# Attention inside a gated-delta-rule stage: both heads of a pair in one step, by row and column groups of the array

## The chip, the core and the metric

The kernel runs on one core of a Trainium2 chip. Its time is the device time of one execution in microseconds (us). Before the change it is 2827.43 us, the median of 3 runs (2822.66 to 2828.75).

The engines are TensorE (PE; its weight loads are listed as PEld), VectorE (DVE), ScalarE (ACT), GpSimd (POOL) and the queue that starts most transfers (SP). Each works through its own instructions in order; they wait for one another by semaphores.

## The reference, cut to what matters

Two transformer-like layers follow each other on x of 1 x 1024 x 1024 (float32). The first mixes tokens in two ways side by side: four heads of a gated delta rule, and eight heads of dilated attention, 64 channels each. The change touches only the attention:

```
for window, dil in ((128, 1), (512, 4), (2048, 16)):
    # query t sees keys t, t-dil, ..., t-window; scores are q.k / 8
    num, den, m = band_attention(...)
out = (w0*num0 + w1*num1 + w2*num2) / (w0*den0 + w1*den1 + w2*den2)   # w_i = exp(m_i - max m)
```

The kernel computes the same as one causal softmax over all keys: scores + strip, where the table strip holds log(how many of the three patterns hold this key), or -1e30. Then

```
x = x + concat(gated_delta_rule(...), attention) @ w_out
```

## The kernel before

**The three stages.** The first stage (0 to about 397 us) projects x. The second (397.9 to about 869 us) runs the gated delta rule and the attention together. The third (the rest) is matmuls with split weights: output projections, feed-forward layers and the second block. The change is within the second stage.

**The second stage** goes over 8 chunks of 128 tokens (`c` = 0..7) for the delta rule. A chunk inverts four 128x128 triangular matrices by six levels: `("corner", l)` is a set of four matmuls LT x T (L1613 on the tensor queue), which DVE masks into U (L1246); `("join", l)` is two sets of four matmuls (L1613), which DVE subtracts from T (L1251) and TT (L1253). After that come `read`, `solve` and `update` (L1697, L1698), the new state St (L1263), and the decays of the next chunk (L1628, the first matmul that needs St). Chunk `c` is worked in turn `i = c // 2`, `p = c % 2`.

**The attention** fills the gaps between the levels. Pair `i` of heads (four pairs) is done in chunks 2i and 2i+1: head `p` of the pair in chunk 2i+p. For each head it goes over the 8 query tiles h = 0..7 of 128 tokens; tile h has h+1 key blocks of 128 (causal). For a tile:

- `("scores", h)`: matmuls of 64 rows (the head's channels, at partitions 64p on) into PSUM banks 3 and 4 (L1721); DVE adds strip, takes the row maximum (L1300) and negates it (L1305); ACT takes the exponential in place in `sm` with row sums (L877).
- `("weigh", h+1)`: TensorE transposes the weights block by block (L1732) and ACT copies them to `pt` (L884). `("weigh", h+2)`: matmuls of the transposed weights (stationary) with values `vb`, 64 columns moving (L1744); DVE takes the reciprocal of the row sum (L1310) and scales the result into `ob` (L1313).
- `heads`, once per pair (after chunk 2i+1): 8 transposes of `ob` (L1706), a copy by ACT into `hh` (L862), the remainder by DVE into `hl` (L1273). `values` at the start of chunk 2i: 8 transposes (L1656) and a copy by ACT into `vb` (L843).

**What sets the order.** The list `ORDER` is written by hand; each engine walks it once per chunk and issues its own part of every stage. Chunks 0, 1, 6 and 7 are written out, chunks 2 to 5 are a loop over i = 1, 2.

```
ORDER = ["values", "turn_back", ("scores", 0), "pairs", "mix", "invert", ("scores", 1), ("weigh", 1)]
for l in range(1, LEVELS):
    ORDER += [("corner", l), ("scores", l + 1), ("join", l), ("weigh", l + 1)]
ORDER += ["begin", "read", ("weigh", 8), "solve", ("weigh", 9), "update", "load", "heads", "gram", "root"]
```

**Around the levels.** `turn_back` and `pairs` need ACT's copies knT and qnT (L847, L849), DVE's LT and AT (L1239, L1241), the masked U and the first T (L1287, L1289). `mix` finishes the delta rule's output of the chunk before (u at L1215, hh at L829, hl at L1220). ACT loads a function table twice in each chunk: for the square root (L870) and for the exponential (L877).

Of the kernel before, what the change touches and what calls it, by code (L numbers as in the profile page):

```python
# [326 lines left out]
def program(nc, a, out):  # L327

    ctx = ExitStack()
    with ctx:  # L330
# [35 lines left out]
        with ExitStack() as z:  # L366
            strip, lmask = sb("strip", [P, S], where=z), sb("lmask", [P, LEVELS + 1, P], where=z)
            ch = sb("ch", [P, 2, 16, P], where=z)
            qkvb = sb("qkvb", [P, 3, S], where=z)
            vb = sb("vb", [P, TT, P], where=z)  # L370
            G = {n: sb(n, [P, GH, P], where=z) for n in
                 "bm E gam kn qn v knT qnT kd qd ke LT AT T TT U u St Sg oz".split()}
            G["og"] = G["u"]
            cc = sb("cc", [P, 2, T_N], where=z)
            oc = sb("oc", [P, 8, GH], where=z)
            sm = sb("sm", [P, 2, S], where=z)
            pt = sb("pt", [P, 2, HALF], where=z)
            ob = sb("ob", [P, TT, P], where=z)
            ac = sb("ac", [P, 4, 16], where=z)
# [90 lines left out]
        def final_bank(a, t):  # L470
# [9 lines left out]
            on_ready ot_mm oh_ready s_mm s_max s_neg s_exp p_mm p_evac pv_mm rd_ready ob_ready obt_mm  # L480
            obh_ready obl_ready
# [31 lines left out]
        ORDER = ["values", "turn_back", ("scores", 0), "pairs", "mix", "invert", ("scores", 1), ("weigh", 1)]  # L513
        for l in range(1, LEVELS):
            ORDER += [("corner", l), ("scores", l + 1), ("join", l), ("weigh", l + 1)]
        ORDER += ["begin", "read", ("weigh", 8), "solve", ("weigh", 9), "update", "load", "heads", "gram", "root"]

        def turns(eng, turn):

            for p in range(2):  # L520
                turn(0, p, p == 0, False)
            with eng.Fori(1, TT // 2 - 1) as i:
                for p in range(2):
                    turn(i, p, False, False)
            for p in range(2):
                turn(TT // 2 - 1, p, False, p == 1)
# [7 lines left out]
        def _(sp):  # L534
# [56 lines left out]
            for i in range(1, 4):  # L591
# [3 lines left out]
                sp.wait_ge(s["s_mm"], 16 * i)  # L595
# [133 lines left out]
        def _(act):  # L729
# [102 lines left out]
            act.sem_inc(s["p_evac"], 2)  # L832
# [3 lines left out]
            def turn(i, p, first_chunk, last):  # L836
                c = 2 * i + p
                g0 = 24 * i + 12 * p
                for stage in ORDER:
# [20 lines left out]
                    elif stage == "heads" and p == 1:  # L860
                        act.wait_ge(s["obt_mm"], i + 1)
                        A(hh[:, bass.ds(4 + i, 1), :].rearrange("p a s -> p (a s)"),  # L862
                          PS[:, 3:5, :].rearrange("p a b -> p (a b)"), ACT.Copy).then_inc(s["obh_ready"], 1)
# [9 lines left out]
                    elif stage[0] == "scores" and stage[1] < 8:  # L873

                        h, n = stage[1], P * (stage[1] + 1)
                        act.wait_ge(s["s_neg"], 16 * i + 8 * p + h + 1)
                        A(sm[:, h % 2, 0:n], sm[:, h % 2, 0:n], ACT.Exp, bias=ac[:, 1, 8 * p + h:8 * p + h + 1],  # L877
                          accum_out=ac[:, 2, 8 * p + h:8 * p + h + 1]).then_inc(s["s_exp"], 1)
                    elif stage[0] == "weigh" and stage[1] <= 8:

                        for g, n in groups(stage[1] - 1):
                            act.wait_ge(s["p_mm"], g0 + g + 1)
                            act.wait_ge(s["pv_mm"], g0 + g + 1)
                            A(pt[:, g % 2, 0:n * P], PS[:, 5 + g % 2, 0:n * P], ACT.Copy).then_inc(s["p_evac"], 1)  # L884
# [164 lines left out]
        def _(dve):  # L1049
# [138 lines left out]
            dve.sem_inc(s["s_max"], 1)  # L1188
            dve.sem_inc(s["ob_ready"], 1)
            dve.sem_inc(s["obl_ready"], 1)  # L1190
# [37 lines left out]
            def turn(i, p, first_chunk, last):  # L1228
                c = 2 * i + p
                g0 = 24 * i + 12 * p  # L1230
                for stage in ORDER:
# [39 lines left out]
                    elif stage == "heads" and p == 1:  # L1271
                        dve.wait_ge(s["obh_ready"], i + 1)
                        TTo(hl[:, bass.ds(4 + i, 1), :].rearrange("p a s -> p (a s)"),  # L1273
                            PS[:, 3:5, :].rearrange("p a b -> p (a b)"),
                            hh[:, bass.ds(4 + i, 1), :].rearrange("p a s -> p (a s)").bitcast(F32),
                            ALU.subtract).then_inc(s["obl_ready"], 1)
# [15 lines left out]
                    elif stage[0] == "scores" and stage[1] < 8:  # L1292

                        h, n, k = stage[1], P * (stage[1] + 1), 8 * p + stage[1]
                        dve.wait_ge(s["s_mm"], 16 * i + k + 1)
                        if h >= 2:
                            dve.wait_ge(s["p_mm"], g0 + groups(h - 2)[-1][0] + 1)

                        V_.memset(small[:, 255:256], 0.0)
                        V_.tensor_tensor_reduce(out=sm[:, h % 2, 0:n],  # L1300
                                                in0=PS[:, 3:5, :].rearrange("p a b -> p (a b)")[:, 0:n],
                                                in1=strip[:, S - n:S], scale=1.0, scalar=-3e38, op0=ALU.add,
                                                op1=ALU.max, accum_out=ac[:, 0, k:k + 1]).then_inc(s["s_max"], 1)
                        dve.wait_ge(s["s_max"], 16 * i + k + 2)
                        TS(ac[:, 1, k:k + 1], ac[:, 0, k:k + 1], -1.0, None, ALU.mult).then_inc(s["s_neg"], 1)  # L1305
                    elif stage[0] == "weigh" and stage[1] >= 2:

                        h, k = stage[1] - 2, 8 * p + stage[1] - 2
                        dve.wait_ge(s["s_exp"], 16 * i + k + 1)
                        V_.reciprocal(ac[:, 3, k:k + 1], ac[:, 2, k:k + 1]).then_inc(s["rd_ready"], 1)  # L1310
                        dve.wait_ge(s["rd_ready"], 16 * i + k + 1)
                        dve.wait_ge(s["pv_mm"], g0 + groups(h)[-1][0] + 3)
                        TS(ob[:, h, 64 * p:64 * p + 64], PS[:, 7, 0:64], ac[:, 3, k:k + 1], None, ALU.mult)\  # L1313
                            .then_inc(s["ob_ready"], 1)
# [172 lines left out]
        def _(pe):  # L1487
# [148 lines left out]
            def mix(c):  # L1636

                pe.wait_ge(s["on_ready"], c + 1)
                pe.wait_ge(s["ob_ready"], 8 * c + 9)
# [3 lines left out]
            pe.sem_inc(s["pv_mm"], 2)  # L1643
# [3 lines left out]
            def turn(i, p, first_chunk, last_chunk):  # L1647
                c = 2 * i + p
                g0 = 24 * i + 12 * p
                for stage in ORDER:  # L1650
                    if stage == "values" and p == 0:

                        pe.wait_ge(pair_loaded, 16 * (i + 1))
                        pe.wait_ge(s["obl_ready"], i + 1)
# [48 lines left out]
                    elif stage == "heads" and p == 1:  # L1703
                        pe.wait_ge(s["ob_ready"], 16 * (i + 1) + 1)
                        for t in range(TT):
                            last = tr(PS[:, 3 + t // 4, (t % 4) * P:(t % 4 + 1) * P], ob[:, t], ident[:])  # L1706
                        last.then_inc(s["obt_mm"], 1)
# [5 lines left out]
                    elif stage[0] == "scores" and stage[1] < 8:  # L1713
                        h, n = stage[1], P * (stage[1] + 1)
                        pe.wait_ge(s["s_max"], 16 * i + 8 * p + h + 1)
                        if p == 0 and h == 0:
                            pe.wait_ge(s["vb_ready"], i + 1)
                        rows_ = slice(64 * p, 64 * p + 64)
                        for lo in range(0, n, HALF):
                            hi = min(n, lo + HALF)  # L1720
                            last = mm(PS[:, 3 + lo // HALF, 0:hi - lo], qkvb[rows_, 0, h * P:h * P + P],  # L1721
                                      qkvb[rows_, 1, lo:hi], start=True, stop=True)
                        last.then_inc(s["s_mm"], 1)
                    elif stage[0] == "weigh":
                        if stage[1] <= 8:
                            h = stage[1] - 1
                            pe.wait_ge(s["s_exp"], 16 * i + 8 * p + h + 1)
                            for g, n in groups(h):
                                pe.wait_ge(s["p_evac"], g0 + g + 1)
                                b0 = 4 * (g - groups(h)[0][0])  # L1730
                                for b in range(n):
                                    last = tr(PS[:, 5 + g % 2, b * P:b * P + P],  # L1732
                                              sm[:, h % 2, (b0 + b) * P:(b0 + b) * P + P], ident[:])
                                last.then_inc(s["p_mm"], 1)
                        if stage[1] >= 2:
                            h = stage[1] - 2
                            pe.wait_ge(s["ob_ready"], 16 * i + 8 * p + h + 1)
                            if h == 0 and not first_chunk:
                                pe.wait_ge(s["og_ready"], c)
                            for g, n in groups(h):  # L1740
# [138 lines left out]
def groups(h):  # L1879

    if h < 4:
        return [(h, h + 1)]
# [26 lines left out]
```

## Time and profile before

| | |
|---|---|
| median of 3 runs | 2827.43 us |
| profiled execution | 2822.73 us, span 2821.1 us |
| PE busy | 2645.8 us (94%) |
| DVE busy | 1640.6 us (58%) |
| ACT busy | 1061.7 us (38%) |
| POOL busy | 121.1 us (4%) |
| mean granted TensorE clock | 0.973 |

A float32 matmul is two records on PE and two on PEld; a transpose is one. The time of one is best read from the chain of work, where a piece is the advance that it made, and not from its duration, since matmuls overlap. The granted clock is a share of the full rate: 1.00 is 2.4 GHz, 0.50 is 1.2 GHz. Chunk boundaries are taken here at L1628, the decays of the next chunk.

### The profile page before, as it was taken

To read this page: it belongs to the slowest core of one execution; us is meant where nothing else is said; L and a number is where in the kernel's file an instruction comes from. 1 tells how busy PE (TensorE), PEld (TensorE's weight loads), DVE (VectorE), ACT (ScalarE), POOL (GpSimd) and SP (SyncE) were. 2 spreads that over 40 slices of the span, in tenths; PEclk is the share of its full clock that TensorE was granted. 3 is DMA by queue.
4 is the path that set the end of the run, shared out by engine and by line. 5 is a ranking of instruction groups with operands and counts; after the bars stand their busy time and mean duration, and the time that the engine had idled before them with its cause. 6 is when DMAs were issued, how large, how long until landed. Compare 5 with 4: busy or idle time off the path is not lost.

```text
span 2821.1 us, 32692 instructions
## 1 busy us (share of the span) xinstructions
PE 2645.8 (94%) x12696; PEld 2168.0 (77%) x12696; DVE 1640.6 (58%) x2458; ACT 1061.7 (38%) x1602; POOL 121.1 (4%) x123
## 2 busy tenths in 40 slices
PE   6999979999997999999999999988999999999998
PEld 5888767777776878878777877776887788788886
DVE  4124335556553566666665888656588864655555
ACT  3123323333332444433544344444433343433332
POOL 1000011112110000000000000000000000000000
PEclk9999989999998999999999999999999999999999
DMA  5222230111104323333223222222332233243332
GB/s 190 91 84 81 75 105 16 38 38 30 38 1 127 97 81 92 98 92 95 89 76 88 85 90 90 83 83 67 91 90 82 83 103 103 75 129 97 97 90 75
DMA packets 299293, 235.05 MB, mean 83 GB/s; under 512 B 8095, under 2 KB 275476, under 8 KB 299028
## 3 DMA queue, kind: packets, MB, share of 16 engines
q1 hardware_dynamic: 293684, 209.57, 25.1%
q0 software_dynamic: 5472, 23.60, 2.1%
q8 instruction: 92, 1.51, 0.2%
q14 instruction: 45, 0.37, 0.0%
HBM read 210.07 MB, written 23.07 MB: 83 GB/s over the span
## 4 chain that ended last, share of the span: by engine, by line
PE 78%; DVE 12%; ACT 4%; issue 3%; DMA 2%; SPq 1%; POOLq 0%; POOL 0%; ACTq 0%; DVEq 0%
PE PS L1781 11%; PE PS L1783 11%; PE PS L1782 11%; PE PS L1503 11%; PE PS L1613 7%; PE PS L1797 5%; PE PS L1798 5%; PE PS L1799 5%; PE PS L1721 3%; DVE wl L1063 3%; PE PS L1744 2%; DVE x L1346 1%; DVE cg L1450 1%; PE PS L1732 1%; ACT wh L737 1%
## 5 line engine op out<-in xcount | busy, mean ns | idle before, releaser
L1781 PE MATMUL PS<-hh,wh 128*128 128x512 f32 x1728 | 686.0, 397 | 6.7 <-DVE hl L1322 4.4
L1063 DVE TENSOR_TENSOR wl<-raw,wh 128x1024 fp32r<-128x1024 f32 x352 | 427.7, 1226 | 447.6 <-ACT wh L737 447.4
L1783 PE MATMUL PS<-hh,wl 128*128 128x512 f32 x1728 | 676.6, 392 | 0.0
L1782 PE MATMUL PS<-hl,wh 128*128 128x512 f32 x1728 | 676.3, 391 | 0.0
L737 ACT ACTIVATE wh<-raw 128x1024 fp32r<-128x1024 f32 x352 | 367.1, 1056 | 536.3 <-PE PS L1799 401.0
L1781 PEld LDWEIGHTS PS<-hh,wh 128*128 128x128 f32 x1728 | 326.8, 189 | 79.2 <-DVE hl L1322 5.5
L1782 PEld LDWEIGHTS PS<-hl,wh 128*128 128x128 f32 x1728 | 326.6, 189 | 71.3 <-issue 4.3
L1783 PEld LDWEIGHTS PS<-hh,wl 128*128 128x128 f32 x1728 | 326.3, 189 | 68.4
L1797 PE MATMUL PS<-fh,wh 128*128 128x512 f32 x864 | 347.9, 403 | 32.3 <-DVE x L1346 25.8
L1346 DVE TENSOR_TENSOR x<-x,PS 128x512 f32<-128x512 f32 x432 | 290.5, 685 | 137.7 <-PE PS L1799 134.8
L1798 PE MATMUL PS<-fl,wh 128*128 128x512 f32 x864 | 341.8, 396 | 0.0
L1799 PE MATMUL PS<-fh,wl 128*128 128x512 f32 x864 | 341.1, 395 | 0.0
L1797 PEld LDWEIGHTS PS<-fh,wh 128*128 128x128 f32 x864 | 165.2, 191 | 79.3 <-DVE x L1346 37.8
L1799 PEld LDWEIGHTS PS<-fh,wl 128*128 128x128 f32 x864 | 165.2, 191 | 35.5
L1798 PEld LDWEIGHTS PS<-fl,wh 128*128 128x128 f32 x864 | 165.3, 191 | 34.8 <-issue 1.2
L1450 DVE SCALAR_TENSOR_TENSOR cg<-cg,par 128x512 f32<-128x512 f32 x240 | 172.0, 748 | 1.3
L1503 PE MATMUL PS<-hh,wh 128*128 128x512 f32 x448 | 140.6, 395 | 7.5 <-DVE hl L1102 3.8
L1503 PE MATMUL PS<-hl,wh 128*128 128x512 f32 x448 | 138.9, 391 | 0.0
L1503 PE MATMUL PS<-hh,wl 128*128 128x512 f32 x448 | 138.5, 391 | 0.0
L877 ACT ACTIVATE sm<-sm,ac 128x128 f32<-128x128 f32 (+3 forms) x64 | 49.6, 776 | 177.9 <-DVE ac L1305 177.8
L1503 PEld LDWEIGHTS PS<-hh,wh 128*128 128x128 f32 x448 | 83.2, 189 | 26.3 <-issue 7.5
L1503 PEld LDWEIGHTS PS<-hh,wl 128*128 128x128 f32 x448 | 84.4, 188 | 18.1
(287 smaller groups left out, 2835.3 us busy)
## 6 DMA issues: line engine op xcount, KB each, us to landing
raw<-in_w_ff SPq DMA_DIRECT2D x128, 512.0 KB, 4.0
raw<-in_w_up SPq DMA_DIRECT2D x88, 512.0 KB, 3.8
raw<-in_w_in SPq DMA_DIRECT2D x60, 512.0 KB, 4.0
raw<-in_w_down SPq DMA_DIRECT2D x44, 512.0 KB, 3.9
raw<-in_w_out SPq DMA_DIRECT2D x32, 512.0 KB, 4.2
qkvz_s<-st POOLq DMA_DIRECT2D x16, 512.0 KB, 2.9
ch<-qkvz_s SPq DMA_DIRECT2D x8, 1024.0 KB, 5.7
qkvb_s<-st POOLq DMA_DIRECT2D x12, 512.0 KB, 2.9
```

The costliest lines, as they stand in the source:

```text
L737: A(whs(slot), raw[:, k % 2], ACT.Copy).then_inc(s["w_hi"], 1)
L1063: TTo(wls(slot), raw[:, k % 2], whs(slot).bitcast(F32), ALU.subtract).then_inc(s["w_lo"], 1)
L1346: TTo(x[:, t, span(a_)], x[:, t, span(a_)], PS[:, bank, :], ALU.add).then_inc(s["x_done"], 1)
L1450: STT(c, cg[:, 2 + q, i:i + HALF], w, c, ALU.mult, ALU.add).then_inc(s["c_tap"], 1)
L1503: last = mm(acc(bank)[:, t * HALF:(t + 1) * HALF], w(slot)[:, cut], h[:, kk, t * HALF:(t + 1) * HALF], start=kk == order[0] and n == 0, st ...
L1613: last = mm(heads(bank)[:, h], left[:, h], right[:, h], start=start, stop=stop)
L1781: mm(bank, wh[:, k % 4, cut], hh[:, kk, span(a_)], start=kk == 0, stop=False)
L1782: mm(bank, wh[:, k % 4, cut], hl[:, kk, span(a_)], start=False, stop=False)
L1783: last = mm(bank, wl[:, k % 4, cut], hh[:, kk, span(a_)], start=False, stop=kk == KT - 1)
L1797: mm(bank, wh[:, (k + m) % 4, cut], fh[:, f], start=m == 0, stop=False)
L1798: mm(bank, wh[:, (k + m) % 4, cut], fl[:, f], start=False, stop=False)
L1799: last = mm(bank, wl[:, (k + m) % 4, cut], fh[:, f], start=False, stop=m == 1)
```

## The change

Both heads of a pair are now done in every chunk, for half of the query tiles. `TILES` names the tiles: 4, 7, 0, 3 in an even chunk, 5, 6, 1, 2 in an odd one, so each chunk still has 36 blocks (18 for either head). `e` = 0, 1 is the head. `j` = 0..3 is the tile's place in the chunk, and a tile over 512 keys wide has two steps `m`, so there are 6 steps in a chunk.

- Scores: two matmuls of a step, head 0 in rows 0 to 63 of the array and head 1 in rows 64 to 127, into banks 3 and 4.
- The weights are scaled by the reciprocal of the row sum ahead of the transposes, by two more ACT copies for each tile (stage `even`); the tiles take turns in `sm` and in `raw` (which holds weights in the other stages only).
- The value matmuls are turned round: `vb` (64 columns) is stationary, `pt` (128 columns) moves, and the heads write partitions 0 to 63 and 64 to 127 of one bank. Their result stands by channels; stage `send` copies it to `hh` (ACT) and the remainder to `hl` (DVE). The stage `heads`, the buffer `ob` and the scaling into it are gone.
- The loop over i is written out.

```diff
-        ORDER = ["values", "turn_back", ("scores", 0), "pairs", "mix", "invert", ("scores", 1), ("weigh", 1)]
-        for l in range(1, LEVELS):
-            ORDER += [("corner", l), ("scores", l + 1), ("join", l), ("weigh", l + 1)]
-        ORDER += ["begin", "read", ("weigh", 8), "solve", ("weigh", 9), "update", "load", "heads", "gram", "root"]
+        ORDER = ["values", "turn_back", ("scores", 0, 0), "pairs", "mix", "invert", ("scores", 0, 1), ("even", 0)]
+        ORDER += [("corner", 1), ("scores", 1, 0), ("join", 1), ("turn", 0, 0)]
+        ORDER += [("corner", 2), ("scores", 1, 1), ("weigh", 0, 0), ("join", 2), ("even", 1), ("turn", 0, 1)]
+        ORDER += [("corner", 3), ("weigh", 0, 1), ("join", 3), ("send", 0), ("turn", 1, 0)]
+        ORDER += [("corner", 4), ("scores", 2, 0), ("weigh", 1, 0), ("join", 4), ("even", 2), ("turn", 1, 1)]
+        ORDER += [("corner", 5), ("scores", 3, 0), ("weigh", 1, 1), ("join", 5), ("even", 3), ("send", 1), ("turn", 2, 0)]
+        ORDER += [("corner", 6), ("weigh", 2, 0), ("join", 6), ("send", 2), ("turn", 3, 0)]
+        ORDER += ["begin", "read", ("weigh", 3, 0), "solve", ("send", 3), "update", "load", "gram", "root"]
+        TILES = (4, 7, 0, 3), (5, 6, 1, 2)
+        def at_step(j, m):
+            return 2 * j + m if j < 2 else 2 + j
+        def keys(p, j, m):
+            n = P * (TILES[p][j] + 1)
+            return m * HALF, min(n, (m + 1) * HALF), n
+        def soft(j):
+            return sm[:] if j % 2 == 0 else raw[:]
...
 # ACT
+                    elif stage[0] == "scores" and stage[2] == last_of(stage[1]):
+                        act.wait_ge(s["s_neg"], 4 * c + j + 1)
+                        for e in range(2):
+                            A(soft(j)[:, e, 0:n], soft(j)[:, e, 0:n], ACT.Exp, bias=ac[:, 1, 2 * j + e:2 * j + e + 1],
+                              accum_out=ac[:, 2, 2 * j + e:2 * j + e + 1]).then_inc(s["s_exp"], 1)
+                    elif stage[0] == "even":
+                        act.wait_ge(s["rd_ready"], 4 * c + j + 1)
+                        for e in range(2):
+                            A(soft(j)[:, e, 0:n], soft(j)[:, e, 0:n], ACT.Copy, scale=ac[:, 3, 2 * j + e:2 * j + e + 1])\
+                                .then_inc(s["s_scaled"], 1)
+                    elif stage[0] == "turn":
+                        for e in range(2):
+                            A(pt[:, e, 0:hi - lo], PS[:, 5 + e, 0:hi - lo], ACT.Copy).then_inc(s["p_evac"], 1)
+                    elif stage[0] == "send":
+                        A(hh[:, GH + i, at:at + P], PS[:, 7, 0:P], ACT.Copy).then_inc(s["b_hi"], 1)
...
 # DVE
+                    elif stage[0] == "even":
+                        dve.wait_ge(s["s_exp"], 8 * c + 2 * j + 2)
+                        V_.reciprocal(ac[:, 3, 2 * j:2 * j + 2], ac[:, 2, 2 * j:2 * j + 2]).then_inc(s["rd_ready"], 1)
+                    elif stage[0] == "send":
+                        dve.wait_ge(s["b_hi"], 4 * c + j + 1)
+                        TTo(hl[:, GH + i, at:at + P], PS[:, 7, 0:P], hh[:, GH + i, at:at + P].bitcast(F32), ALU.subtract)\
+                            .then_inc(s["b_lo"], 1)
...
 # PE
+                        for e in range(2):
+                            rows_ = slice(64 * e, 64 * e + 64)
+                            last = mm(PS[:, 3 + e, 0:hi - lo], qkvb[rows_, 0, at:at + P], qkvb[rows_, 1, lo:hi], start=True, stop=True)
...
+                        pe.wait_ge(s["p_evac"], 2 * (6 * c + at_step(j, m) + 1))
+                        if m == 0 and 4 * c + j:
+                            pe.wait_ge(s["b_lo"], 4 * c + j)
+                        for b in range(lo, hi, P):
+                            for e in range(2):
+                                ch_ = slice(64 * e, 64 * e + 64)
+                                last = mm(PS[ch_, 7, 0:P], vb[:, b // P, ch_], pt[:, e, b - lo:b - lo + P], start=b == 0, stop=b + P == n)
```

On DVE, from the end of `mix` (hl, L1220 before, L1245 after) to the masked U of the first level, in chunk 1. Names in brackets are the semaphores waited for; ISA rows are the maximum with its read-out. Before:

```order
L1220 TENSOR_TENSOR hl<-u,hh 128x4x128 [waits oh_ready]
L1299 MEMSET small 128x1 [waits s_mm]
L1300 ISA sm,ac<-PS,strip 128x256
L1300 ISA ac 128x1
L1305 TENSOR_SCALAR ac<-ac 128x1 [waits s_max]
L1246 TENSOR_TENSOR U<-PS,lmask 128x512 [waits lev_l]
```

and of the changed kernel (here chunk 2):

```order
L1245 TENSOR_TENSOR hl<-u,hh 128x4x128 [waits oh_ready]
L1322 MEMSET small 128x1 [waits s_mm]
L1323 ISA sm,ac<-PS,strip 128x128
L1323 ISA ac 128x1
L1322 MEMSET small 128x1
L1323 ISA sm,ac<-PS,strip 128x128
L1323 ISA ac 128x1
L1330 TENSOR_TENSOR ac<-ac 128x2 [waits s_max]
L1331 TENSOR_SCALAR ac<-ac 128x2 [waits v_chain]
L1335 RECIPROCAL ac<-ac 128x2 [waits s_exp]
L1271 TENSOR_TENSOR U<-PS,lmask 128x512 [waits lev_l]
```

A reciprocal that waits for s_exp (ACT's exponentials of the same tile) now stands ahead of U; before, the reciprocal of a tile stood two stages later.

On ACT, chunk 1, from the exponentials of the widest early tiles to the copies of transposed weights that follow them. Before:

```order
L877 ACTIVATE sm,ac<-sm,ac 128x384 [waits s_neg]
L884 ACTIVATE pt<-PS 128x256 [waits pv_mm,p_mm]
L877 ACTIVATE sm,ac<-sm,ac 128x512 [waits s_neg]
L884 ACTIVATE pt<-PS 128x384 [waits pv_mm,p_mm]
L877 ACTIVATE sm,ac<-sm,ac 128x640 [waits s_neg]
L884 ACTIVATE pt<-PS 128x512 [waits pv_mm,p_mm]
```

and of the changed kernel:

```order
L907 ACTIVATE pt<-PS 128x512 [waits pv_mm,p_mm]
L907 ACTIVATE pt<-PS 128x512
L890 ACTIVATE raw,ac<-raw,ac 128x896 [waits s_neg]
L890 ACTIVATE raw,ac<-raw,ac 128x896
L897 ACTIVATE raw<-raw,ac 128x896 [waits rd_ready]
L897 ACTIVATE raw<-raw,ac 128x896
L907 ACTIVATE pt<-PS 128x256 [waits pv_mm,p_mm]
L907 ACTIVATE pt<-PS 128x256
```

The copy of step (0, 1) to `pt`, 256 wide, now stands behind two exponentials and two scalings of tile 1, each 896 wide; before, one exponential stood between two copies.

On the tensor queue, chunk 1, corner 2 to join 3 of the changed kernel (L1640 is L1613 of before, L1746 scores, L1757 transposes, L1771 values):

```order
L1640 MATMUL PS<-T,LT 128x128 x3
L1746 MATMUL PS<-qkvb 128x384 [waits s_max]
L1746 MATMUL PS<-qkvb 128x384
L1771 MATMUL PS<-pt,vb 64x128 [waits og_ready,b_lo,p_evac]
L1771 MATMUL PS<-pt,vb 64x128 x7
L1640 MATMUL PS<-U,TT 128x128 [waits lev_tt,lev_u]
...
L1757 MATMUL PS<-ident,sm 128x128 [waits p_evac,s_scaled]
L1757 MATMUL PS<-ident,sm 128x128 x3
L1640 MATMUL PS<-T,LT 128x128 [waits lev_t]
L1640 MATMUL PS<-T,LT 128x128 x3
L1771 MATMUL PS<-pt,vb 64x128 [waits p_evac]
L1771 MATMUL PS<-pt,vb 64x128 x3
```

The value matmuls of step (0, 1), which wait for p_evac (the copy to `pt`), stand ahead of join 3; before, the value matmuls stood between a join and the next corner, right behind the transposes of the tile after them.

## Rows read from the trace of the kernel before

**Rows 1.** The page: busy time, share of the span, instructions.
```profile
PE 2645.8 (94%) x12696; PEld 2168.0 (77%) x12696; DVE 1640.6 (58%) x2458; ACT 1061.7 (38%) x1602; POOL 121.1 (4%) x123
```
**Rows 2.** Windows by chunk, chunks 1, 3 and 4: PE, PEld, DVE, ACT, POOL busy; clock.
```profile
455.60:512.90 57.30, 52.08 (x355) 43.50 (x355) 32.08 (x83) 20.41 (x40) 11.28 (x9) 0.94 0.16 47
570.90:629.40 58.50, 54.04 (x354) 45.34 (x354) 32.64 (x83) 20.41 (x40) 11.29 (x9) 0.91 0.15 46
629.40:687.40 58.00, 54.28 (x371) 45.38 (x371) 34.25 (x84) 22.34 (x42) 10.99 (x9) 0.94 0.07 18
```
**Rows 3.** Chain of work, chunk 3, levels 5 and 6: start, us, what.
```profile
607.57 0.95 PE PS L1613 x8
608.52 1.70 PE PS L1721 x4
610.22 1.98 PE PS L1613 x16
612.20 0.66 PE PS L1732 x6
612.86 1.06 PE PS L1744 x10
...
614.86 1.91 PE PS L1721 x4
616.78 1.09 PE PS L1613 x8
```
**Rows 4.** Timeline of PEld at the last of these: its idle time in brackets.
```profile
616.70 0.97 PEld L1613 LDWEIGHTS PS<-TT,U 128*128 128x128 f32 x8 [0.76 <-issue]
```
**Rows 5.** Chain of work, chunk 5, start of the chunk to its first level.
```profile
686.62 0.70 DVE St L1263
...
687.36 1.14 PE PS L1628 x2
...
698.64 1.75 DVE hl L1220
```
**Rows 6.** Timeline of PE: the first corner of chunk 4 and of chunk 5.
```profile
642.02 1.82 PE L1613 MATMUL PS<-T,LT 128*128 128x128 f32 x8 [1.39 <-DVE T L1289]
...
698.77 1.16 PE L1613 MATMUL PS<-T,LT 128*128 128x128 f32 x8 [1.39 <-DVE T L1289]
```
**Rows 7.** Windows of 2 us, chunk 5 (columns as in group 2).
```profile
697.40:699.40 2.00, 0.63 (x5) 0.63 (x6) 1.97 (x3) 0.38 (x1) 2.00 (x2) 1.00 0.47 134
701.40:703.40 2.00, 2.00 (x7) 1.03 (x6) 0.94 (x5) 0.33 (x3) 2.00 (x3) 0.50 0.28 70
707.40:709.40 2.00, 2.00 (x11) 1.12 (x11) 0.95 (x3) 0.00 (x0) 0.00 (x0) 1.00 0.00 0
```
**Rows 8.** Timeline of DVE, chunk 4: a maximum of 512 columns, and what follows.
```profile
651.93 0.69 DVE L1300 CUSTOM_DVE_ANT_0 sm<-PS,strip 128x512 f32<-128x512 f32 x1
...
652.67 0.15 DVE L1305 TENSOR_SCALAR ac<-ac 128x1 f32<-128x1 f32 x1
```
**Rows 9.** Groups of ACT by shape, second stage: count, busy, mean ns.
```profile
L884 ACT ACTIVATE pt<-PS 128x512 f32<-128x512 f32 x48 | 28.7, 597 | 31.7 <-PE PS L1744 25.6 <-PE PS L1732 5.1
L877 ACT ACTIVATION_READ_ACCUMULATOR sm<-sm,ac 128x1 f32 x64 | 11.9, 187 | 0.0
L877 ACT ACTIVATE sm<-sm,ac 128x1024 f32<-128x1024 f32 x8 | 9.2, 1149 | 28.9 <-DVE ac L1305 28.9
...
L884 ACT ACTIVATE pt<-PS 128x256 f32<-128x256 f32 x16 | 6.1, 381 | 18.9 <-PE PS L1732 18.9
...
L877 ACT ACTIVATE sm<-sm,ac 128x512 f32<-128x512 f32 x8 | 5.8, 722 | 22.7 <-DVE ac L1305 22.7
```
**Rows 10.** The page: ACT's copy from SBUF to SBUF, 1024 columns.
```profile
L737 ACT ACTIVATE wh<-raw 128x1024 fp32r<-128x1024 f32 x352 | 367.1, 1056 | 536.3 <-PE PS L1799 401.0
```
**Rows 11.** Timeline, the stage's end: heads, and the way to the last mix.
```profile
861.76 1.02 ACT L862 ACTIVATE hh<-PS 128x1024 fp32r<-128x1024 f32 x1 [0.51 <-PE PS L1706]
...
864.33 0.18 DVE L1281 RECIPROCAL oc<-oc 128x4 f32<-128x4 f32 x1 [0.29 <-ACT oc L870]
```

More of the change, by code:

```diff
@@ L872, in turn @@
                         mix(c - 1)
[L873 to L884, printed above, removed]
+                    elif stage[0] == "scores" and stage[2] == last_of(stage[1]):
+                        j = stage[1]
+                        n = keys(p, j, 0)[2]
+                        act.wait_ge(s["s_neg"], 4 * c + j + 1)
[3 more added lines that the diff above has]
+                    elif stage[0] == "even":
+                        j = stage[1]
+                        n = keys(p, j, 0)[2]
+                        act.wait_ge(s["rd_ready"], 4 * c + j + 1)
[3 more added lines that the diff above has]
+                    elif stage[0] == "turn":
+                        lo, hi, _ = keys(p, *stage[1:])
+                        g = 6 * c + at_step(*stage[1:])
+                        act.wait_ge(s["p_mm"], g + 1)
+                        if g:
+                            act.wait_ge(s["pv_mm"], g)
+                        for e in range(2):
+                            A(pt[:, e, 0:hi - lo], PS[:, 5 + e, 0:hi - lo], ACT.Copy).then_inc(s["p_evac"], 1)
+                    elif stage[0] == "send":
+                        j = stage[1]
+                        at = TILES[p][j] * P
+                        act.wait_ge(s["pv_mm"], 6 * c + at_step(j, last_of(j)) + 1)
+                        A(hh[:, GH + i, at:at + P], PS[:, 7, 0:P], ACT.Copy).then_inc(s["b_hi"], 1)
@@ L1291, in turn @@
                             mix_low(c - 1)
[L1292 to L1314, printed above, removed]
@@ L1702, in turn @@
                         load(c + 1, 1 - p, i + p)
[L1703 to L1707, printed above, removed]
                     elif stage == "gram" and not last_chunk:
@@ L1712, in turn @@
                         mix(c - 1)
[L1713 to L1716, printed above, removed]
-                            pe.wait_ge(s["vb_ready"], i + 1)
[L1718 to L1722, printed above, removed]
-                        last.then_inc(s["s_mm"], 1)
-                    elif stage[0] == "weigh":
[L1725 to L1740, printed above, removed]
-                                pe.wait_ge(s["p_evac"], g0 + g + 3)
-                                b0 = 4 * (g - groups(h)[0][0])
-                                for b in range(n):
-                                    last = mm(PS[:, 7, 0:64], pt[:, g % 2, b * P:b * P + P],
-                                              vb[:, b0 + b, 64 * p:64 * p + 64], start=b0 + b == 0, stop=b0 + b == h)
-                                last.then_inc(s["pv_mm"], 1)
```

87 lines of the change are left out of this document (55 added, 32 removed).

## The prediction

> **What bounds the kernel now.** I read the page first: PE is busy 94% of the span, ACT 38% [rows 1]. Then the windows by chunk of the stage that changes: a chunk takes 57.3 to 58.5 us, and PE is busy for 52 to 54 of them at a mean clock of 0.91 to 0.94, DVE for 32 to 34, ACT for 20 to 22 [rows 2]. Then the chain of work inside a chunk. From the second level on it is PE without a gap: a corner takes 0.95, a join 1.98, the scores of 7 key blocks 1.70 and of 8 blocks 1.91 (so about 0.21 and 0.2125 for each block), a transpose 0.11 (6 in 0.66), a value matmul 0.21 (5 in 1.06) [rows 3]. At the start of a chunk the chain goes through other engines: the decays start at 687.36, DVE's hl of `mix` at 698.64 [rows 5], and the first corner starts at 698.77 (11.4 us on) after 1.39 us of waiting for T [rows 6]. There the clock falls from 1.00 (2.4 GHz) through 0.50 (1.2 GHz) and is back at 1.00 some 6 us later; PE had been busy 0.63 of 2 us before it fell [rows 7].
>
> So the attention's matmuls count in full where PE never waits, and at two places something else counts: DVE's order at the first level, and from now on whatever lies between a score and its value matmul.
>
> **An odd chunk before, at the high clock.** Join 1 can start once U is masked: hl of `mix` ends 13.0 us on (698.64 + 1.75), a maximum of 256 columns and U take 1.3, so 14.3. From there PE works in a row: five joins 9.9, the last 1.09, five corners 4.75, `read` and `solve` 1.9, `update` 2.7 (twelve matmuls of 0.21 to 0.24), St and its release 0.74 (686.62 to 687.36 [rows 5]), scores of five tiles 7.4, transposes 3.85, values 7.6: 40.1. Sum 54.4. Odd chunks took 57.7 in the mean of four (57.3 to 58.5, two of the rows [rows 2]), so the fall of the clock costs 3.3. In an even chunk the first corner comes 1.2 later (642.02 in the chunk from 629.44, 12.6 on [rows 6]; `heads` and `values` stand ahead), so 55.6 against 58.0 measured: 2.4. One fall of the clock costs about 3 us.
>
> **PE's own work after.** A chunk still has 36 blocks. Scores go from 8 steps to 6. If the two row groups never overlap, scores take 36 x 0.2125 + 6 x 0.21 = 8.9 instead of 9.3; if they overlap fully, 5.1. A float32 matmul is two records one after the other, and a step has only one matmul for each head, so I take that the second record of head 0 lies beside the first of head 1: three record times for four, 18 x 0.32 + 6 x 0.21 = 7.0. No row shows two groups at work at once; three quarters stands between the ends. A value matmul now moves 128 columns like those of a corner, 0.24 each: 8.6 without overlap, 4.3 with; in a row of blocks head 0 and head 1 can alternate, so I take 4.3, and 0.4 for each of 6 steps for filling and for the switch of tile form: 6.7 instead of 7.6. That switch is in the trace: behind scores PEld stands idle 0.76 us to the end of the last score matmul [rows 4] and the set takes 1.09 instead of 0.95 [rows 3]; before, values were in the same form as what stood around them, now they are not. The transposes stay. From join 1 on, PE's row is then 35.0 us instead of 40.1 in an odd chunk (scores of three steps 3.2 for 7.4, the rest having moved ahead of join 1; values 0.9 less), 35.3 in an even one.
>
> The Trainium skill (TensorEngine Tiling (Array Packing), Theoretical Speedup) gives up to 2x for two tiles, and under Key Properties says that a change of tiling mode drains the TensorE. The idle 0.76 us of PEld agrees with the drain; no row here shows the speedup. By its 2x the scores would be 5.1 instead of my 7.0, 15 us less over 8 chunks if all of it lay on the path.
>
> **What the new order makes wait.** Durations: a maximum of 512 columns with its read-out advances DVE by 0.74 (651.93 to 652.67) [rows 8], two heads take 1.5; an exponential of 512 columns takes 0.72 and the read-out the rest to 0.81, one of 1024 takes 1.29 [rows 9], so 1.14 at 896 and 1.02 at 768; a scaling copy of 1024 columns has the form of wh<-raw, 1.06 [rows 10], so 0.95 at 896, 0.85 at 768; copies to `pt` 0.60 and 0.38 [rows 9]. The scaling is new work: 4608 columns, about 5.4 us of ACT per chunk; it counts only where someone waits. The path of an odd chunk (tiles 5, 6, 1, 2), in us from its start:
>
> 1. Scores (0,0) are 4 blocks for both heads, 5.3 to 6.8, and their maxima hold DVE until 8.45, ahead of LT. LT was free to go at 7.4. T ends at 12.1 instead of 11.4, hl of `mix` at 13.75.
> 2. Scores (0,1): two maxima, the larger of them, the negation, to 15.0. ACT: two exponentials of 768, to 17.1. DVE's reciprocal waits for them, and U stands behind it: U ends 18.0. Join 1 starts at 18.05, not 14.3: **+3.75**. PE has a corner and one score step (2.4 us) to do meanwhile and waits the rest.
> 3. Scores (1,1) end at 23.0; maxima to 24.9, exponentials of 896 to 27.2, reciprocal, scalings to 29.4, and only then the copy of step (0,1), to 30.1. PE is through with the values (0,0), join 2, the transposes and corner 3 at 27.75. The values (0,1) stand ahead of join 3, so the inversion waits too: **+2.4**.
> 4. Scores (3,0) end at 41.6, maxima 43.3, exponentials 44.8, the reciprocal behind join 5's TT at 45.75, scalings, `send` 1, copy of step (2,0) 47.85. PE is there at 46.15: **+1.7**.
> 5. `solve` is followed by `update` at once; before, the values of the widest tile (8 x 0.21) covered ACT's copy u. Now PE waits for it: **+0.9**.
>
> Sum for odd chunks: 18.05 + 35.0 + 5.0 = 58.05 against 54.4, +3.6. Even chunks (tiles 4, 7, 0, 3): `values` moves in ahead, and the first scores wait for ACT's copy vb behind the square root, so join 1 is at 19.1 instead of 15.5; the wait of point 3 is 3.15 (1024 columns), that of point 4 1.95, of point 5 0.9: 19.1 + 35.3 + 6.0 = 60.4 against 55.6, +4.8.
>
> **What it gives back otherwise.** `heads` is inside what even chunks were compared with. At the stage's end the square root no longer stands behind hh of `heads` and the reciprocal not behind its hl: from 861.76 to 864.33 it is 2.6 now, about 1.2 without [rows 11]: -1.4. The written-out loop, the pair's load (its last score comes earlier) and `send` (0.3 on ACT and DVE, beside PE) I put at nothing: PE covers them; without that cover `send` would cost 0.5 for each of 4 tiles.
>
> Total at the high clock with one fall as now: 4 x 3.6 + 4 x 4.8 - 1.4 = +32.
>
> **The clock.** PE now idles for 2.4 to 3.2 us at point 3, longer than the 1.39 us that go before the fall now. I take one more fall per chunk at 3 us: +24. Together **+56**: 2822.7 + 56 = 2879 for an execution like the profiled one; the median of the runs is 4.7 above that one, of which I add 3: 2882.
>
> **The rivals.**
> - *The clock falls only once per chunk, as now.* For it: PE has 10 us of unbroken work between points 2 and 3. +32: 2858. Chance 0.17.
> - *The groups don't overlap.* Score steps on the path cost 0.2 to 0.4 more each and value steps 0.35 to 0.75; walked the same way 4.3 more per chunk, +34: 2916. For it: no row shows overlap, and both heads' records stand in one queue. Chance 0.2.
> - *PE stays the bound, and it gets faster.* The place is DVE's U behind the reciprocal, and ACT's copy behind the scalings. If these waits and the later T come to less than PE's row saves (5.1 us per chunk), the sum turns; with none of them 3.2 per chunk of work and 3.5 of `heads` in all with 1.4 at the end are saved: 8 x 3.2 + 3.5 + 1.4 = 30 less, 2797. For it: PE is 94% busy and the work gets less. Against: ACT's and DVE's rows give 8.75 us. Chance 0.13.
> - *It evens out:* half of the walked waits, 2827. Chance 0.05.
>
> **How the numbers follow.** The forecast has 0.45, with its own range 2860 to 2905 (no second fall in some chunks; a third one, at point 4, in others). 2838 to 2925 takes in the single fall and most of the case without overlap, and leaves the two good cases out. This kernel's runs can tell about 0.2% from no change. Slower 0.83, within 0.2% 0.04, faster 0.13.
>
> **What would show it.** In the changed trace: chunks of 61 to 64 us; U of level 1 idle on DVE behind a reciprocal that waits for ACT about 2 us; PE's values of step (0,1) waiting for ACT's `pt` 2 to 3 us; ACT some 5 us busier per chunk; two stretches at 0.50 per chunk; PE's busy time in a chunk lower. The prediction is wrong if a tile's score step is over in half the time of now, if DVE is not late with U, or if the clock stays up.

## The result, and the profile of the changed kernel

The changed kernel takes 2841.82 us, the median of 5 runs (2835.81 to 2844.3), against 2824.82 us before (median of 5 in the same rounds): 1.0055 times as long, with a 95% interval of 1.004 to 1.0071, so +17 us. The forecast of 2882 had the sign right and more than three times the loss; 2842 lies outside its own range of 2860 to 2905. The profiled execution has a span of 2842.6 us and a mean granted clock of 0.963.

The page, busy time of each engine (as in [rows 1]):

```profile
PE 2604.5 (92%) x12664; PEld 2130.3 (75%) x12664; DVE 1631.1 (57%) x2470; ACT 1102.0 (39%) x1694; POOL 121.1 (4%) x123
```

PE has 41 us less to do than in [rows 1] and ACT 40 more, and yet the time is longer: PE now waits. Windows by chunk, chunks 1, 3, 4 and 5 (columns as in [rows 2]):

```profile
463.26:522.56 59.30, 47.20 (x355) 39.07 (x355) 31.79 (x85) 25.96 (x52) 11.29 (x9) 0.88 0.15 45
584.89:643.14 58.25, 46.11 (x354) 38.02 (x355) 31.80 (x85) 25.96 (x52) 11.29 (x9) 0.91 0.15 46
643.14:704.49 61.35, 47.96 (x363) 39.82 (x363) 31.99 (x85) 26.87 (x53) 11.29 (x9) 0.92 0.07 18
704.49:762.68 58.19, 46.05 (x355) 37.97 (x355) 31.81 (x85) 25.95 (x52) 11.29 (x9) 0.91 0.15 46
```

Chunk 3 takes 58.25 us, 0.25 less than before [rows 2], although PE is busy for 46 of them instead of 54. Chunk 1 took 57.3 and now takes 59.3, chunk 4 took 58.0 and now takes 61.35. The second stage goes from 397.86 to 869.12 us before and from 398.60 to 887.73 now: 471.3 and 489.1 us, +17.8. The two profiled executions differ by 21.5 us; the other 3.7 lie in stages that the change doesn't touch (0.7 in the first, and 2.9 in the third, which took 1952.0 and 1954.9). The length of the second stage in the profiled execution is therefore given below beside each median.

The chain of work in chunk 3, from the end of `mix` to the first value matmuls of the second tile (start, us, what):

```profile
596.50 1.68 DVE hl L1245
...
599.36 0.99 DVE ac L1331
600.35 0.02 issue
600.37 1.96 ACT sm L890 x4
602.33 0.02 issue
602.35 0.04 DVE ac L1335
602.38 0.05 issue
602.43 0.68 DVE U L1271
603.11 0.04 issue
603.15 3.78 PE PS L1640 x16
606.94 1.71 PE PS L1757 x8
608.64 1.14 PE PS L1640 x8
609.78 0.85 PE PS L1746 x4
610.63 1.02 PE PS L1771 x16
611.65 2.00 PE PS L1640 x16
...
615.51 1.03 ACT raw L897
616.53 0.55 ACT pt L907 x2
617.08 0.04 issue
617.13 0.66 PE PS L1771 x8
617.78 1.98 PE PS L1640 x16
619.76 0.87 PE PS L1757 x8
620.64 0.89 PE PS L1640 x8
621.53 0.63 PE PS L1746 x4
622.16 1.02 PE PS L1771 x16
```

[Rows 3] had PE in every row. Here the chain leaves PE twice, and three more times later in the chunk, each time through ACT's copy to `pt` (the values at 627.72, 633.29 and 636.66). At 600.37 it goes through ACT's exponentials (L890), DVE's reciprocal (L1335) and U, and join 1 starts at 603.15. At 615.51 it goes through ACT's scaling and copy, and the values of step (0,1) start at 617.13. The joins at 611.65 and 617.78 still take 2.0; the one at 603.15 takes 3.78; the granted clock there is 0.50 (602.9 to 606.9).

What PE waited for in the second stage (line, what it waited for, us in total, times, longest):

```profile
PE PS L1771 <- ACT pt L907: 34.1, 24, 2.9
PE PS L1640 <- DVE U L1271: 16.8, 8, 2.3
PE PS L1640 <- DVE T L1308: 15.3, 8, 2.2
```

The first two are the new waits: 51 us, 6.4 in a chunk.

### The profile page after: what moved, and what is told of

The parts are those of the page before. It is cut to its first block, busy times and chain, and to the rows that moved or that the text cites. A ratio compares the mean times of both kernels' runs of the same rounds, so it can differ in the third digit from the quotient of the medians.

```text
span 2842.6 us, 32214 instructions
## 1 busy us (share of the span) xinstructions
PE 2604.5 (92%) x12664; PEld 2130.3 (75%) x12664; DVE 1631.1 (57%) x2470; ACT 1102.0 (39%) x1694; POOL 121.1 (4%) x123
## 4 chain that ended last, share of the span: by engine, by line
PE 73%; DVE 14%; ACT 6%; issue 4%; DMA 1%; SPq 1%; POOLq 0%; POOL 0%; ACTq 0%; DVEq 0%
PE PS L1807 11%; PE PS L1809 11%; PE PS L1808 11%; PE PS L1530 11%; PE PS L1823 5%; PE PS L1640 5%; PE PS L1824 5%; PE PS L1825 5%; DVE wl L1091 3%; DVE x L1373 1%; DVE cg L1477 1%; PE PS L1771 1%; PE PS L1757 1%; ACT wh L753 1%; DVE uc L1378 1%
## 5 line engine op out<-in xcount | busy, mean ns | idle before, releaser
L1808 PEld LDWEIGHTS PS<-hl,wh 128*128 128x128 f32 x1728 | 327.5, 190 | 71.7 <-issue 4.6
L1823 PE MATMUL PS<-fh,wh 128*128 128x512 f32 x864 | 347.1, 402 | 31.7 <-DVE x L1373 25.2
L1530 PEld LDWEIGHTS PS<-hl,wh 128*128 128x128 f32 x448 | 85.1, 190 | 18.4
```

The lines of the kernel that those rows point to most:

```text
L1530: last = mm(acc(bank)[:, t * HALF:(t + 1) * HALF], w(slot)[:, cut], h[:, kk, t * HALF:(t + 1) * HALF], start=kk == order[0] and n == 0, st ...
L1808: mm(bank, wh[:, k % 4, cut], hl[:, kk, span(a_)], start=False, stop=False)
L1823: mm(bank, wh[:, (k + m) % 4, cut], fh[:, f], start=m == 0, stop=False)
```

## The experiments

All times are medians; the ratio is to the kernel before in the same rounds.

**1. The loop written out, and nothing else** (in the kernel before):

```diff
-            for p in range(2):
-                turn(0, p, p == 0, False)
-            with eng.Fori(1, TT // 2 - 1) as i:
...
+            for c in range(TT):
+                turn(c // 2, c % 2, c == 0, c == TT - 1)
```

> The kernel before with nothing changed but the loop over i, which is written out as in the changed kernel. If written-out code were part of the loss (instruction fetch, other gaps between chunks), this would be 5 us or more slower than before. My theory puts it at nothing: 2825 us, within 3.

2823.86 us, ratio 1.0002 (0.9993 to 1.0012), second stage 471.3 us as before. The loop is worth nothing, as it was put down.

**2 to 4. The two waits moved away.** The reciprocal of the first tile behind the next score step, the copies to `pt` ahead of the next tile's scalings, and both:

```diff
-... ("scores", 0, 1), ("even", 0)]
-... ("corner", 1), ("scores", 1, 0), ("join", 1) ...
+... ("scores", 0, 1)]
+... ("corner", 1), ("scores", 1, 0), ("even", 0), ("join", 1) ...
```

```diff
-... ("join", 2), ("even", 1), ("turn", 0, 1)]
-... ("join", 5), ("even", 3), ("send", 1), ("turn", 2, 0)]
+... ("join", 2), ("turn", 0, 1), ("even", 1)]
+... ("join", 5), ("send", 1), ("turn", 2, 0), ("even", 3)]
```

> The changed kernel with stage even 0 moved behind the scores (1, 0): DVE masks U of level 1 before it waits for ACT's exponentials. Theory of waits: the 1.5 to 2.1 us that PE waits for U in each chunk go, 8 x 2 = 16 us, so about 2826 us, and the idle time of join 1's first matmuls behind DVE's U falls below 0.5 us per chunk. Rival (the tensor queue's own work and the low clock set the pace at the start of a chunk, the wait only moves): less than 5 us, 2837 to 2842.

> The changed kernel with ACT's copies of steps (0, 1) and (2, 0) to pt (and send 1) ahead of the scalings of tiles 1 and 3. Theory of waits: of the 2.2 to 2.9 us in front of the values (0, 1) some 2.0 go and of the 1.4 to 1.7 in front of the values (2, 0) some 1.1: 3 us per chunk, 24 in all, about 2818 us, faster than the kernel before. Rival (the exponentials, not the scalings, set these waits): 1 us per chunk, 2834.

> Both moves together. Theory of waits: the gains add, 16 + 24, about 2802 us, clearly below the kernel before. Rival (one wait takes the place of the other, since tile 1's exponentials come earlier only if join 1 does): under 30 us in all, 2812 or more.

| kernel | median | ratio (95%) | second stage |
|---|---|---|---|
| changed | 2841.8 | 1.0055 (1.004 to 1.0071) | 489.1 |
| reciprocal later | 2822.57 | 0.9996 (0.9986 to 1.0006) | 473.3 |
| copies first | 2809.77 | 0.9946 (0.9934 to 0.9959) | 453.9 |
| both | 2788.46 | 0.9874 (0.9859 to 0.9889) | 431.1 |

Each move gives more than forecast, 19 and 32 us, and together 53, the sum of the two within the intervals. The waits go with them: U's falls from 16.8 to 0.7 us with the first move, that for `pt` from 34.1 to 3.5 with the second; with both they are 4.3 and 3.5, 43 us less in all. Part of the rest is the clock: in kernel 4 it is 1.00 in every chunk from 23 us after the chunk's start on, where the changed kernel has second falls (below). With both, PE's timeline at the same place (chunk 3; idle time before a row in brackets) reads:

```profile
583.65 1.06 PE L1640 MATMUL PS<-T,LT 128*128 128x128 f32 x8
584.65 0.66 PE L1771 MATMUL PS<-pt,vb 128*64 128x128 f32 x8
585.49 1.16 PE L1640 MATMUL PS<-U,TT 128*128 128x128 f32 x8 [0.17 <-DVE U L1271]
```

Corner, values and join follow one another with 0.17 us between them. So the step in two heads at once is the faster one, 36 us below the kernel before, and what made the changed kernel slow was where two small operations stood in DVE's and ACT's order.

**5, 6 and 12. The overlap taken away.** The values head by head (5); both heads' scores in rows 0 to 63, so that head 1 gets head 0's scores (6, work as much as before but one row group); both (12):

```diff
-                        for b in range(lo, hi, P):
-                            for e in range(2):
+                        for e in range(2):
+                            for b in range(lo, hi, P):
```

```diff
-                            rows_ = slice(64 * e, 64 * e + 64)
+                            rows_ = slice(0, 64)
```

> The changed kernel with the value matmuls of a step done for all blocks of head 0 and then for all of head 1, so that neighbours in the tensor queue are in the same column group. Theory A (the two column groups work at the same time, and full overlap is why the kernel came out 40 us below my forecast): the value step of 4 blocks goes from 1.03 us (chain) to about 1.9, and with the steps that have cover taken out (those ahead of a wait for ACT) 2.5 us per chunk show, 2862 us. Rival (the groups do not overlap; the value matmul is short because its weights are half as wide): no change, 2842.

> The changed kernel with the scores of both heads taken from partitions 0 to 63 (so head 1 gets the scores of head 0: this part of the computation is changed), which puts both matmuls of a step in the same row group; same number, same shapes. Theory A (row groups overlap fully, not three quarters as I took): a step of 4 blocks goes from 1.06 to 1.91 us; on the path are (0,0), (1,1), (2,0) and (3,0), 2.7 us per chunk, 2863 us. Three-quarters theory of the prediction: 1.48 to 1.91, half of that, 2852. No overlap: 2842.

> The changed kernel with both edits against overlap: value matmuls by head, and the scores of both heads from the same rows (head 1 gets head 0's scores; this part of the computation is changed). The two cost 13 and 22 us alone; if they add, 2877. The prediction's rival without overlap stood 34 us above its own three-quarters value, which with full overlap as the base makes more: 2842 + 49 = 2891. If the waits for ACT cover one behind the other, below 2870.

Values by head: 2855.22 us, ratio 1.0114 (1.0097 to 1.0131), second stage 504.4. One row group: 2863.86 us, 1.0149 (1.0134 to 1.0164), 509.8. Both: 2879.39 us, 1.0203 (1.0186 to 1.022), second stage 528.5, which is 39.4 more than in the changed kernel; the two alone make 15.3 and 20.7, so they add up, or nearly. The chain of work of kernel 6, a score step of 4 blocks for either head, and then one of 3:

```profile
593.80 1.91 PE PS L1746 x4
...
613.02 1.48 PE PS L1746 x4
```

and the chain of the changed kernel at the first of these steps:

```profile
590.22 1.06 PE PS L1746 x4
```

The same four records take 1.06 in two row groups and 1.91 in one; 1.91 is also what 8 blocks took in [rows 3]. For 3 blocks it is 0.85 and 1.48. So the groups overlap almost fully, though a head has only one matmul of two records. For the values, kernel 5 in its chain:

```profile
613.86 1.51 PE PS L1771 x16
```

against 1.02 for the same 16 records when the heads alternate. By head they still take less than the 1.9 that 8 matmuls of 128 columns would at 0.24 each; whether the last block of head 0 overlaps the first of head 1, or the rows of a 64-column weight load are quicker, no run here tells.

**7. No scaling of the weights** (ACT's two copies of `even` left out, so the result is not divided by the row sums):

```diff
-                        for e in range(2):
-                            A(soft(j)[:, e, 0:n], soft(j)[:, e, 0:n], ACT.Copy, scale=ac[:, 3, 2 * j + e:2 * j + e + 1])\
-                                .then_inc(s["s_scaled"], 1)
+                        act.sem_inc(s["s_scaled"], 2)
```

> The changed kernel without the ACT copies that scale the weights (the semaphore is raised instead, so the attention's result is not divided by its row sums: this part is left out). Theory of waits: the scalings count only at the values (0, 1) and (2, 0), 2.0 + 1.1 us per chunk, 25 us, about 2817; about the time with the copies first. Rival (the scaling is 5.4 us per chunk of ACT that all lies on the path): 43 us less, 2799.

2810.09 us, ratio 0.9958 (0.9944 to 0.9971), second stage 455.4. That is 31.7 us below the changed kernel, where moving the copies ahead gave 32. The scaling, 5 us of ACT in a chunk, costs what it costs only by standing ahead of the copies that PE waits for.

**8. The first maxima behind LT and AT** (kernel 4, with `pairs` ahead of the first scores and, for the even chunks, `values` behind `turn_back`):

```diff
-        ORDER = ["values", "turn_back", ("scores", 0, 0), "pairs", "mix" ...
+        ORDER = ["turn_back", "values", "pairs", ("scores", 0, 0), "mix" ...
```

> Both moves of the reordered kernel (2788), and in addition the stages values and scores (0, 0) behind turn_back and pairs. ACT then copies knT and qnT before vb, and DVE masks LT and AT before the first maxima. Theory: in even chunks pairs no longer stand behind ACT's vb, 1.4 us gained of which the maxima, now ahead of u and U, take back 0.8; in odd chunks a loss of up to 1 us: between 2784 and 2791. Rival (the first corner is set by the maxima wherever they stand before it): slower, 2791 to 2796.

2798.56 us, 0.9916 (0.9901 to 0.993), second stage 445.2: 10 us more than kernel 4, 14 in the stage, and more than either expectation. PE's wait for T grew from 15.1 to 17.7 us, and the transposes now wait 9.0 us for ACT's scalings of the first tile (1.8 in kernel 4). In chunk 3 DVE starts T 12.8 us after the chunk's start, where kernel 4 has 10.4: the maxima now stand between AT and u. Point 1 of the forecast put the later T down to these maxima; ahead of LT they are in the better place.

**9 to 11. Added matmuls against the fall of the clock at the first corner.** Matmuls ident x ident into bank 6, which nobody reads there, ahead of corner 1 (8, and 4 more ahead of scores (1,0)); in kernel 4 (9), in the changed kernel (10), and 5 ahead of corner 1 in the kernel before (11):

```diff
                     elif stage[0] == "corner":
+                        if stage[1] == 1:
+                            for _ in range(8):
+                                mm(PS[:, 6, 0:P], ident[:], ident[:], start=True, stop=True)
...
+                        if (j, m) == (1, 0):
+                            for _ in range(4):
+                                mm(PS[:, 6, 0:P], ident[:], ident[:], start=True, stop=True)
```

> The kernel with both moves, and where PE waits at the start of a chunk (1.8 us for T, 1.2 us for the maxima of step (0, 1)) 8 and 4 matmuls of ident with ident into a free bank, whose result nobody reads. They do no work of the kernel; they only keep PE busy. Theory (the one fall of the clock per chunk costs about 3 us, since join 1 and the transposes run at half rate on the path): with PE busy the granted clock stays at 1.00 there and 20 us go, 2768. Rival (at that place DVE and ACT set the pace, the fall costs nothing): 2786 to 2790, or more where the added matmuls run at half rate.

> The changed kernel with the same added matmuls. If the fall costs what it does in the kernel before (3 us per chunk, the basis of my term for the clock), 2818 to 2822. If the wait for U hides most of it, since join 1 starts late anyway, only join 1 and the transposes behind it count, 2 us per chunk: 2826. Nothing: 2842.

> The kernel before with 5 such matmuls ahead of the first corner of each chunk (it waits 1.4 us there). My working took a fall as 2.4 to 3.3 us per chunk: 2802 if the clock stays up; 2825 if the fall costs nothing or is not avoided.

| kernel | median | ratio (95%) | second stage |
|---|---|---|---|
| 9: both moves, filled | 2783.52 | 0.9863 (0.9848 to 0.9879) | 429.1 |
| 10: changed, filled | 2837.72 | 1.0053 (1.0041 to 1.0065) | 482.4 |
| 11: before, filled | 2810.13 | 0.9953 (0.994 to 0.9967) | 447.9 |

Windows by chunk of kernel 11, chunks 3 and 4:

```profile
561.65:615.99 54.34, 50.37 (x364) 42.30 (x365) 32.22 (x83) 20.41 (x40) 11.30 (x9) 1.00 0.16 49
615.99:671.50 55.51, 52.28 (x380) 44.02 (x380) 34.16 (x84) 22.35 (x42) 11.00 (x9) 1.00 0.07 19
```

The clock is 1.00 (2.4 GHz) throughout these two, and they take 54.3 and 55.5 us; the forecast's sums for the high clock were 54.4 and 55.6. The second stage is 23.4 us shorter, 2.9 in a chunk: in the kernel before, one fall cost what the forecast put down for it (3.3 and 2.4). In the whole time only 14 of these 23 us arrive; the third stage of that execution took 1962.6 us, where it took 1949 to 1958 in the others, with nothing in it changed. What it lost there stays open.

In the changed kernel the filling kept the clock up in chunk 0 only. From chunk 1 on it fell all the same, so there kernel 10 doesn't measure what the fall costs. A window of 5 us and a row of PE's timeline, chunk 3:

```profile
598.00:603.00 5.00, 5.00 (x24) 5.00 (x25) 2.37 (x7) 0.97 (x2) 0.00 (x0) 0.50 0.00 2
...
597.81 2.07 PE L1640 MATMUL PS<-U,TT 128*128 128x128 f32 x8 [3.08 <-DVE U L1271]
```

PE is ready for join 1 earlier and waits longer for U (23.6 us in all instead of 16.8), and in chunk 3 the clock falls during that wait. Join 1 starts 18.27 us after the chunk's start (18.26 without the filling) and takes 3.78 us as before. Chunks 3 to 7 are as long as in the changed kernel to 0.1 us; the 6.7 us less in the stage lie in chunks 0 to 2 (4.5, 1.1 and 1.0). In kernel 4 the filling holds: the clock is at 1.00 in chunks 3 and 4 (0.93 and 0.94 before), but these take 51.7 and 53.5 us against 52.0 and 54.8, and the stage is 2.0 shorter. That is the rival's case, in which DVE and ACT set the pace at this place and the fall costs next to nothing. Kernel 9 is the fastest of all, 41 us below the kernel before.

## Why the prediction was right in its sign and wrong in its size

**Point 1, the first maxima ahead of LT: smaller.** In chunk 3 hl of `mix` ends 13.3 us after the chunk's start (598.18 from 584.89), forecast 13.75, 13.0 before.

**Point 2, U behind the reciprocal: right.** Join 1 was forecast at 18.05 us from the chunk's start and stands at 18.26 (603.15 from 584.89); in the even chunk 4 at 19.54, forecast 19.1. DVE's timeline shows the wait of about 2 us:

```profile
602.35 0.17 DVE L1335 RECIPROCAL ac<-ac 128x2 f32<-128x2 f32 x1 [2.01 <-ACT sm L890]
```

**Points 3 and 4, values behind the scalings: right, a little large.** PE's timeline, chunk 3, and chunk 2 for an even one:

```profile
617.13 0.66 PE L1771 MATMUL PS<-pt,vb 128*64 128x128 f32 x8 [2.17 <-ACT pt L907]
...
633.29 0.66 PE L1771 MATMUL PS<-pt,vb 128*64 128x128 f32 x8 [1.39 <-ACT pt L907]
```

```profile
556.58 0.44 PE L1771 MATMUL PS<-pt,vb 128*64 128x128 f32 x4 [2.86 <-ACT pt L907]
...
574.48 0.44 PE L1771 MATMUL PS<-pt,vb 128*64 128x128 f32 x4 [1.69 <-ACT pt L907]
```

Forecast were 2.4 and 1.7, and 3.15 and 1.95. Kernels 2, 3 and 4 show that these waits set the time.

**Point 5, `update` waits for u: right.** 0.73 instead of 0.9. The profile calls this wait ahead of L1724 "issue"; in chunk 3 ACT's u ends at 639.26 and L1724 starts at 639.36. **The stage's end:** from the end of the last `update`'s matmuls with u (880.57, before 859.95) to the first matmul of the third stage (887.73, before 869.12) it is 7.2 us, where it was 9.2: -2.0 instead of -1.4. (The terms of the forecast's PE row before add up to 39.9, not 40.1; nothing hangs on the 0.2.)

**The step that failed first: "three record times for four, 18 x 0.32" and "0.4 for each of 6 steps".** The forecast chose three quarters between no overlap and full overlap, with no row for it. Measured are 1.06, 0.85 and 0.63 for 4, 3 and 2 blocks of both heads, so 0.21 for each block and 0.21 for a step. In an odd chunk, from join 1 on, the three score steps take 2.3 where 3.2 was put down. The six value steps take 5.1 (1.02, 0.66, 1.02, 0.88, 0.66, 0.88) where 6.7 was put down: the charge for filling and form was mostly not there. That makes 2.5 us a chunk and 20 in all. The Trainium skill had the better number (TensorEngine Tiling (Array Packing), Theoretical Speedup: up to 2x for two tiles); kernel 6 against the changed kernel gives 1.8x for a step of 4 blocks. I named the rule, gave its price, and then went by a thought about queued records. The rival without overlap was wrong: kernel 12 comes nearest to it (its value steps, 1.51 for 4 blocks, are still short of 1.9), and costs 37.6 us more than the changed kernel. The forecast put it 34 above its own step times, which were themselves 20 too dear. Kernel 12's 2879 is close to the forecast of 2882, but that is chance: the forecast got there with three quarters of the overlap and falls of the clock that were priced too high.

**The second step that failed: "one more fall of the clock per chunk at 3 us".** Windows of 2 us (columns as in [rows 2]), chunk 2 and then chunk 3, each first at the wait for the copy of step (0,1) and then 4 us on:

```profile
554.60:556.60 2.00, 0.02 (x2) 0.02 (x2) 0.00 (x0) 1.93 (x4) 0.00 (x0) 1.00 0.00 0
558.60:560.60 2.00, 2.00 (x11) 2.00 (x10) 0.97 (x3) 0.00 (x0) 0.00 (x0) 0.50 0.00 0
...
614.90:616.90 2.00, 0.06 (x1) 0.00 (x0) 0.69 (x1) 2.00 (x4) 0.00 (x0) 1.00 0.00 0
618.90:620.90 2.00, 2.00 (x20) 2.00 (x20) 1.57 (x3) 0.23 (x1) 0.00 (x0) 1.00 0.00 0
```

In both PE does next to nothing for 2 us. In chunk 2 the clock is at 1.2 GHz afterwards, in chunk 3 it stays at 2.4 GHz. It fell there in chunks 0, 1, 2, 4 and 6 (twice in chunk 0), and not in 3, 5 and 7. And a second fall is cheaper than 3 us. It lasts under 4 us, and the chain of work of chunk 1 has in it

```profile
494.89 0.66 PE PS L1771 x8
495.55 2.91 PE PS L1640 x16
498.46 1.59 PE PS L1757 x8
500.05 0.89 PE PS L1640 x8
```

where chunk 3 has 1.98 and 0.87: 1.65 us. Six such falls make 10 us, not 24. The first fall costs 2.9 in chunk 3 (3.78, 1.71 and 1.14 instead of 2.00, 0.87 and 0.89), and by the same pieces 2.3 to 3.0 in chunks 0, 1, 2, 5 and 7. In the even chunks 4 and 6 it costs only 1.7 (2.94 and 1.64 in chunk 4), since part of it lies in DVE's chain, where PE waits anyway. That is 19.7 in all; the 3.3 and 2.4 that the forecast kept from before make 22.8, so 3 less. These prices are read from the chain. The one check by a run is chunk 0 of kernel 10, where the first fall and one of the two later ones are gone: it is 4.5 us shorter, and the pieces make 3.0 and 1.65.

So the rival of a single fall (2858) was right about the clock in three of the eight chunks.

**The sum again.** From 56: 20 less for the steps, 14 for the second falls, 3 for the first falls, 1 for the stage's end, 4 for smaller waits (points 3 to 5); 3 more for the later join 1. That leaves 17. Measured are 17.8 in the stage. Taken chunk by chunk, the same terms come within 0.8 us of what each chunk gained or lost, chunk 0 too: it takes 64.7 us where the other even ones take 61.3 to 62.3, and has one later fall more.

**The rival "PE stays the bound, and it gets faster"** gave 2797 if the two waits were away. Kernel 4, which takes them away, has 2788. So the mechanism was there. That the sizes agree to 9 us is in part luck: with the steps as short as measured the rival's own sum is 20 lower, 2777, and kernel 4 still has the later T. The condition on which it hung, that DVE and ACT let PE through, is what failed in the changed kernel.

## What to carry to other kernels

When several engines walk one hand-written order, a change that saves time on the engine that bounds can lose it through two small operations in another engine's queue: look at what stands ahead of each result that the bounding engine waits for, and put a copy that someone waits for ahead of work that has time. Here that was worth 53 us, three times the change's own loss. When no row shows an overlap, measure it by itself or give each end its own case, and don't settle on a middle: the middle for the scores and the charge on top for the values were both too dear. A fall of the clock counts only as far as the matmuls under it lie on the path, so its price is read from the pieces of the chain and not carried from one place to another.

## What the runs showed of the hardware that I had not expected

- One float32 matmul of two records for each head, in row groups 0 to 63 and 64 to 127, overlaps with the other's almost fully: 1.06 us instead of 1.91 for 4 blocks, 0.85 instead of 1.48 for 3.
- PE's idle time alone did not tell whether the clock falls: after 2.16 us of waiting in chunk 1 it fell, after 2.17 us at the same place in chunk 3 it didn't.
- A small DVE operation took six times its usual time. DVE's timeline, twice the negation of 128 x 2 values in chunk 3:

```profile
599.36 0.98 DVE L1331 TENSOR_SCALAR ac<-ac 128x2 f32<-128x2 f32 x1
...
611.96 0.17 DVE L1331 TENSOR_SCALAR ac<-ac 128x2 f32<-128x2 f32 x1
```

At the first, GpSimd was at work:

```profile
599.27 1.04 POOL L708 TENSOR_TENSOR ke<-kn,E 128x512 f32<-128x512 f32 x1
600.27 1.04 POOL L711 TENSOR_TENSOR Sg<-St,gam 128x512 f32<-128x512 f32 x1
```

The small one ended where GpSimd changed from the one operation to the next, at 600.3. In all eight chunks the first negation takes 0.98 us or more (1.20 in chunk 0) and the other three 0.17. That it waited for GpSimd fits this and wasn't tested by a run. It stands on the path to U, so some 0.8 us of join 1's delay in each chunk are this operation's.
